# A weight stream split in two parts: moving the upper part from GpSimd to ScalarE

## The reference

```python
def reference(x, c, ctx, ...):
    x = first_block(x, c, ctx, ...)      # modulated norm; windowed attention with rope and
                                         # context, a gated convolution, gates, mixing; then
                                         # 8 heads pick 16 experts each of 16384 per token;
                                         # final rmsnorm
    return second_block(x, mem_2, ...)   # layer 0: mLSTM mixer; layer 1: pooling mixer;
                                         # each then attends to a memory of 256 rows and
                                         # runs a squared-ReLU MLP of width 4096,
                                         # a layer norm after every part
```

## Time and profile before

| | |
|---|---|
| median of 3 runs | 3497.38 us (3495.84 to 3499.48) |
| the profiled execution | 3496.58 us, its span 3494.8 us |
| mean granted TensorE clock | 0.928 of full speed |
| TensorE busy | 84% of the span |
| VectorE, ScalarE, GpSimd busy | 65%, 26%, 53% |
| DMA engines from 640 to 2000 us | near 100%, about 420 GB/s |

### The profile page before, as it was taken

The page is one execution under the profiler, slowest core; times in us unless marked ns, Lnnn a source line. Parts: engine busy times, 40 slices in busy tenths (PEclk is TensorE's granted clock), DMA queues, the critical chain, the costliest instruction groups (busy, mean ns, idle before and its releaser), DMA issues. The chain is left out here.

```text
span 3494.8 us, 33128 instructions
## 1 busy us (share of the span) xinstructions
PE 2945.1 (84%) x10628; PEld 1938.5 (55%) x10628; DVE 2257.4 (65%) x3761; ACT 926.1 (26%) x2350; POOL 1856.1 (53%) x1099
## 2 busy tenths in 40 slices
PE   6889898877778877888877779979899975889998
PEld 5667676632333323444433267657678864667886
DVE  7793464376666667776766583675855577586556
ACT  2115402233433333333333322221200012220001
POOL 2544375464444444666554264254577763557874
PEclk9899899999999999999999989989999987999998
DMA  5531122699999999999999811011122220112221
GB/s 216 185 113 55 43 79 73 241 421 419 413 418 412 412 422 409 391 389 399 390 422 418 341 66 55 31 60 61 60 90 96 91 72 12 61 60 93 94 96 55
DMA packets 126107, 719.21 MB, mean 206 GB/s; under 512 B 13200, under 2 KB 16400, under 8 KB 60176
## 3 DMA queue, kind: packets, MB, share of 16 engines
q0 software_dynamic: 73728, 536.90, 37.4%
q1 hardware_dynamic: 46560, 161.18, 13.4%
q10 hardware_dynamic: 5680, 19.40, 1.5%
HBM read 715.33 MB, written 2.10 MB: 205 GB/s over the span
## 5 line engine op out<-in xcount | busy, mean ns | idle before, releaser
L712 PE MATMUL psum<-slots,acc 128*128 128x512 f32 x2048 | 1016.2, 643 | 267.9 <-ACT acc L1167 267.4
L398 POOL TENSOR_TENSOR whi<-w,zeros 128x1024 fp32r<-128x1024 f32 x277 | 548.1, 1979 | 883.1 <-PE psum L469 566.4
L428 POOL DMA_INDIRECT slots<-in_experts,consts x512 | 564.1, 1102 | 675.0 <-PE psum L712 603.5
L1719 DVE SCALAR_TENSOR_TENSOR arena<-slots,work 128x1024 f32<-128x1024 f32 x512 | 663.2, 1295 | 400.1 <-DMA slots<-in_experts,consts 383.1
L712 PEld LDWEIGHTS psum<-slots,acc 128*128 128x128 f32 x2048 | 393.7, 202 | 868.5 <-ACT acc L1167 462.3
L401 POOL TENSOR_TENSOR wlo<-w,whi 128x1024 fp32r<-128x1024 f32 x277 | 718.2, 2593 | 21.7
L467 PE MATMUL psum<-xhi,whi 128*128 128x512 f32 x1104 | 451.5, 409 | 8.7 <-POOL wlo L401 5.6
L468 PE MATMUL psum<-xlo,whi 128*128 128x512 f32 x1104 | 441.8, 400 | 0.0
L469 PE MATMUL psum<-xhi,wlo 128*128 128x512 f32 x1104 | 440.5, 399 | 0.0
L467 PE MATMUL psum<-yhi,whi 128*128 128x512 f32 (+1 forms) x736 | 300.1, 408 | 49.9 <-POOL ylo L453 20.7
L468 PE MATMUL psum<-ylo,whi 128*128 128x512 f32 (+1 forms) x736 | 296.2, 402 | 0.0
(11 more groups left out here) (266 smaller groups left out, 3671.3 us busy)
## 6 DMA issues: line engine op xcount, KB each, us to landing
w<-in_stream SPq DMA_DIRECT2D x277, 512.0 KB
arena<-in_wmod SPq DMA_DIRECT2D x4, 2048.0 KB, 17.8
arena<-in_wmod ACTq DMA_DIRECT2D x8, 1024.0 KB, 6.1
acc<-in_wmod ACTq DMA_DIRECT2D x8, 1024.0 KB, 8.3
slots<-in_experts,consts POOLq DMA_INDIRECT x512
xres<-in_xT SPq DMA_DIRECT2D x1, 2048.0 KB, 15.3
outT<-xres SPq DMA_DIRECT2D x8, 256.0 KB, 2.0
consts<-in_consts SPq DMA_DIRECT2D x1, 1056.0 KB, 5.2
```

Of the source, the lines that this page charges most:

```text
L398: pool.tensor_tensor(hi, w32[:, s, :], zeros[:, :].broadcast_to((P, 1024)), ALU.add)\
L428: pool.indirect_dma_start(out=slots[p % SLOTS], out_offset=None, in_=a["experts"], in_offset=bass.IndirectOffsetOnAxis(ap=indices[:, p:p + ...
L712: mm = pe.matmul(bank(4 + half), diag[:, p % 2, :], v[:, half * T:(half + 1) * T], start=(c == 0), stop=(c == PICKS - 1))
L1719: dve.scalar_tensor_tensor(dot_out, slots[p % SLOTS][:, 0:D], 1.0, tokens[:, p // PICKS, :], ALU.mult, ALU.mult, accum_out=inner[:, c:c + ...
```

## The change

GpSimd no longer writes the upper part. ScalarE does, with a copy from `w32` into `whi`, and signals `w_upper`; the waits for the load and for `tile_done` move with it. GpSimd waits for `w_upper` to reach n + 1 and writes the lower part alone. Since ScalarE's list is written by hand, a call `upper(n + m + RING)` is put behind the instruction that reads product m in every stage: the upper part of a tile is written four tiles ahead, behind ScalarE's copy of the product of the tile whose slot it takes. In the start the first four uppers stand behind the root of the second norm.

```diff
-            def split_tile(s, n, nth, reused):
-
-                pool.wait_ge(w_loaded[s], nth * 16)
-                if reused:
-                    pool.wait_ge(tile_done, n + 1 - RING)
+            def split_tile(s, n):
+
+                pool.wait_ge(sem("w_upper"), n + 1)
                 hi = whi[:, s, :, :].rearrange("p k n -> p (k n)")
                 lo = wlo[:, s, :, :].rearrange("p k n -> p (k n)")
-                pool.tensor_tensor(hi, w32[:, s, :], zeros[:, :].broadcast_to((P, 1024)), ALU.add)\
-                    .then_inc(sem("w_upper"), 1)
-                pool.wait_ge(sem("w_upper"), n + 1)
                 pool.tensor_tensor(lo, w32[:, s, :], hi.bitcast(F32), ALU.subtract).then_inc(w_split, 1)
...
+            def upper(n, turn=0):
+
+                if n >= NTILES:
+                    return
+                s = n % RING
+                act.wait_ge(w_loaded[s], turn * 64 + 16 * (n // RING + 1))
+                if n >= RING:
+                    act.wait_ge(tile_done, turn * 16 + (n + 1 - RING))
+                act.activation(whi[:, s, :, :].rearrange("p k n -> p (k n)"), w32[:, s, :], ACT.Copy)\
+                    .then_inc(sem("w_upper"), 1)
...
                     act.activation(work[:, k % 2, 0:cols], src(k), ACT.Square).then_inc(sem("squared"), 1)
+                    if also is not None:
+                        also(k)
...
             root(1)
+            for m in range(RING):
+                upper(m)
...
             for i in range(5):
                 raw(i, o + 1 + i)
+                upper(n + i + RING)
...
                 attn_slot(i)
+                upper(SECTIONS[f"conv{i}"][0] + RING)
...
                 attn_slot(12 + i)
+                upper(n + i + RING)
             for i in range(28, 34):
                 attn_slot(i)
...
+            for m in range(KB):
+                upper(first_tile("branch") + m + RING)
...
+            squares(2, lambda k: xres[:, k, :], ready=lambda k: wait_read(act, SECTIONS["mix"][1] + k),
+                    also=lambda k: upper(first_tile("mix") + k + RING))
...
                         copy_product(mem_raw[:, m % 2, :], o + m, CT)
+                    upper(n + m + RING)
...
                 copy_product(lraw[:, m % 2, 3:3 + T], o + m)
+                upper(n + m + RING)
                 if m:
                     silu(m - 1)
...
+            def upper_after(n, per=1):
+                return lambda k: upper(n + k // per + RING) if k % per == per - 1 else None
+
+            n, o = SECTIONS["lout"]
+            post_norm(4, 0, read_of(o), also=upper_after(n))
...
-                    post_norm(7, 3, pooled)
+                    post_norm(7, 3, pooled, also=upper_after(n, 4))
...
                     copy_product(xq[:, m, :], oo)
+                    upper(n + m + RING)
                     if m % 2:
...
                 for k in range(4):
                     relu(o + k, layer == 0 and k < 2, k)
+                    upper(n + k + RING)
+
+                def hidden_group(half, turn):
+                    for k in range(4):
+                        relu(o + 4 + 12 * half + k, False, 4 + 4 * half + k, turn)
+                        upper(n + 4 + 8 * half + k + RING, turn)
+                    for k in range(4):
+                        upper(n + 8 + 8 * half + k + RING, turn)
+
                 with act.Fori(0, 3) as g:
...
+                post_norm(ni + 2, 3 * layer + 2, read_of(o + 88), last=(layer == 1), also=upper_after(n + 60, 2))
```

More of the change, by code:

```diff
@@ L980, in _, with squares @@
             step = Steps(act, "act_step")
-            def squares(ni, src, cols=T, ready=None):
+            def upper(n, turn=0):
[7 more added lines that the diff above has]
+                    .then_inc(sem("w_upper"), 1)
+            def squares(ni, src, cols=T, ready=None, also=None):
                 for k in range(KB):
@@ L1063, in _ @@
             act.activation(v_tok.rearrange("p t n -> p (t n)"), bank(7), ACT.Copy).then_inc(sem("values_copied"), 1)
+            upper(n + 5 + RING)
             def attn_exp(u):
@@ L1236, in _ @@
             act.activation(mrow, mrow, ACT.Ln, bias=1.0).then_inc(sem("gate_rows"), 1)
+            upper(n + 8 + RING)
             for m in range(9):
@@ L1241, in _ @@
                     copy_product(work[:, m % 2, :], o + 9 + m)
+                    upper(n + 9 + m + RING)
                 if m:
@@ L1264, in _ @@
                     free(act.activation(lsig[:, j, :], bank(oo % RING), ACT.Sigmoid), oo)
+                    upper(n + 2 * h + j + RING)
                 for j in range(2):
@@ L1270, in _, with post_norm @@
             head_root(3)
-            def post_norm(ni, j, ready, last=False):
-                squares(ni, lambda k: acc[:, k, :], ready=ready)
+            def post_norm(ni, j, ready, last=False, also=None):
+                squares(ni, lambda k: acc[:, k, :], ready=ready, also=also)
                 root(ni)
@@ L1286, in _ @@
                 if layer:
-                    o = SECTIONS["pool"][1]
+                    n, o = SECTIONS["pool"]
                     def scale_pooled(k):
@@ L1331, in _ @@
                 x_copy(3)
-                post_norm(ni + 1, 3 * layer + 1, read_of(SECTIONS[f"xo{layer}"][1]))
+                n, o = SECTIONS[f"xo{layer}"]
+                post_norm(ni + 1, 3 * layer + 1, read_of(o), also=upper_after(n))
                 act.wait_ge(sem("affine_done"), 8 * (ni + 2))
@@ L1351, in _ @@
                     relu(o + k, layer == 0 and k < 2, k)
-                with act.Fori(0, 3) as g:
-                    for half in range(2):
-                        for k in range(4):
-                            relu(o + 4 + 12 * half + k, False, 4 + 4 * half + k, g)
-                for k in range(4):
-                    relu(o + 76 + k, False, 28 + k)
-                post_norm(ni + 2, 3 * layer + 2, read_of(o + 88), last=(layer == 1))
+                    upper(n + k + RING)
[5 more added lines that the diff above has]
+                        upper(n + 8 + 8 * half + k + RING, turn)
+                with act.Fori(0, 3) as g:
+                    hidden_group(0, g)
+                    hidden_group(1, g)
+                hidden_group(0, 3)
+                post_norm(ni + 2, 3 * layer + 2, read_of(o + 88), last=(layer == 1), also=upper_after(n + 60, 2))
         @block.vector
```

14 lines of the change are left out of this document (6 added, 8 removed).

## The result

The changed kernel takes 3346.76 us (median of 4 runs, 3342.16 to 3349.42) beside 3496.61 us for the kernel before (4 runs, 3494.16 to 3499.48). The ratio is 0.957, with a 95% interval of 0.9553 to 0.9586: 150 us faster. The forecast was 3382, its range 3350 to 3442.

The account below looks back on a forecast made before the run. VectorE, slowed beside GpSimd's weight splits, was taken to delay the serial stages between stretches bound by TensorE or DMA. Stage terms summed to -115 us from 3497.4, giving 3382 us, range 3350 to 3442.

Parts of the forecast that it names:

- the LSTM: LSTM projections: three of VectorE's four instructions per tile become free, TensorE sets the pace; -19 us (-7 to -21).
- the MLP starts: Start of both MLPs: a hidden tile takes about 4.2 us on VectorE and TensorE's waits go; -20 us (-6 to -22).
- L1984's median: Sign: this 128x512 VectorE instruction's median falls from 1546 ns to near 700, its maximum staying near 2900.
- L583's wait: Sign: TensorE's wait for VectorE before the LSTM's value tiles, 15.3 us there, should go.
- L505's sum: Sign: TensorE's total wait for the sums of the later norms falls from 52.8 to about 22 us.
- L614's wait: Sign: TensorE's wait for the attention's turned probabilities, 29.1 us, falls to about half.
- the halving: Attention: half of 19 us of TensorE's waiting and some of the half clock after it go; -10 us.
- the bound of -17: Large end of the attention term, which was -10 us with bounds -4 to -17.
- the reading of the DMA share: Expert stage, between gathers: DMA at 0.98 against 1.00 read as 7 us lost; term -4 us (-12 to +5).
- half of it: Rival: each lower part hits VectorE's critical instruction, or two blocked instructions per tile remain; -50 us, 3447; chance 0.18.
- Slower: Rival: weights come late behind ScalarE where TensorE waits for a bank freed by a copy; +37 us, 3534; chance 0.06.
- the large ends together: All terms at their large bounds: -151 us, 3346 us; times below the range got chance 0.05.

Follow-up runs that it names:

- fills: Changed kernel with two GpSimd fills of 0.95 us and two one-column additions before each lower part, no tensor moved: 3384.5 us, ratio 0.969.
- repeated upper part: Changed kernel in which GpSimd writes the upper part again into the lower part's place before subtracting, for all tiles: 3456.3 us, ratio 0.9897.
- putting it back in this stretch alone: Changed kernel with GpSimd writing the upper part again for tiles 6 to 21 only (rotations, attention beside conv tiles): 3357.7 us, ratio 0.9617.
- the addresses: Kernel before the change with 4 unused bytes per partition behind `zeros`, moving the tensors behind it: 3475.6 us, ratio 0.9961.
- the order alone: Changed kernel, but ScalarE only signals with a one-column copy at its upper parts' places and GpSimd makes both parts: 3468.0 us, ratio 0.9932.
- pads of 0 and 60 bytes: Changed kernel with unused bytes per partition behind `zeros`: 0 gives 3346.8 us, 60 gives 3347.8; 4 gives 3323.4, 12 gives 3325.6.

## Why the prediction was right, and where it was wrong

Right was the mechanism and its place. VectorE was slow because GpSimd's reads blocked it; the change removes half of these instructions; the stages in which VectorE ends last gain. The pair of fills and repeated upper part is the test: with GpSimd held about as long and ScalarE's work the same, the instruction that reads cost 72 us more than the fills. The terms for the rotations, the LSTM, the norms, the cross attentions, the MLP starts and the pool are all within 3 us of what was measured, and of the signs named ahead all came but one: L1984's median fell to 694 ns, its maximum stayed, L583's wait went, L505's sum fell to 25.4 us (22 expected), ScalarE takes 1.05 us for a tile, the lower part holds TensorE for 4.4 us. The one that did not come is L614's wait, which was to fall to about half and fell to a quarter, 7.7 of 29.1 us.

The step that failed in the attention is the halving. The prediction said "Halving 19 us of waiting and some of the half clock after it". Half the blocked instructions need not leave half the wait. The term was 10 us for both attention stretches; 29.2 were gained, 27.2 of them beside the conv tiles. A stretch that VectorE bounds gets shorter with VectorE until TensorE bounds it, and here the change crosses that point: VectorE's busy time fell from 109.6 to 78.7 us against TensorE's 95.2. All of the waiting went, and with it all of the half clock. GpSimd's second instruction accounts for 11.1 of the 27.2 us, as putting it back in this stretch alone showed; the fills, which take as long and do not read the weights, give back 0.7. Where the other 16 us come from is open, the order and the addresses being worth some 5 to 6 each. Still, the trace of before had the end value. In its window above the granted clock is 0.91 over 122.3 us, 11 us lost, and the table of waits of that stretch has

```profile
PE psum L614 <- DVE arena L1553: 19.4, 6, 4.8
```

122.3 - 19.4 - 11 is 92 us, a possible gain of 30. This estimate is a few us too large, since part of the half clock ran while TensorE waited: TensorE was busy for 102.9 us, 7.7 more than the 95.2 at the full clock, and 122.3 - 19.4 - 7.7 is the 95.2 that came out. For the bound of -17 the prediction shows no working. For the LSTM and the MLP starts the prediction had done exactly this comparison, VectorE's time for a tile against TensorE's 5.6 us, and came within 1 us. That closeness is in part luck, as the next paragraph shows. A slip of its sum at the MLP start has no effect: at the 0.233 us of its own rows 5 us hold 21 matmuls, not 23.

The order has a share in the gain too, which the prediction took for nothing: 24 us in all. In the LSTM projections the order alone gives 9.6 us, half of the 19.1 that the prediction had put down to fewer blocked instructions. At the MLP starts the order alone costs 7.1 us, so the division of the work gave some 28 where 21 were measured and 20 forecast. The terms came out right as sums of two effects, one of which was not in the forecast: that is luck in the size, though not in the sign. How the two add up within a stage was not taken apart further.

The step that failed between the gathers is the reading of the DMA share. The prediction took 0.98 against 1.00 as 7 us of loss in 360. The column beside it in the earlier trace rows says 393 GB/s against 413, 5% and not 2%, which over 360 us is 17.4 us; 17.2 were gained, and the stretch now runs at 415 GB/s. That the two agree so closely is luck, for it hangs on the stretch that one compares with: over all of the first gathers, 640 to 1398 us, the kernel before moved 408 GB/s (and 404 from 640 to 2000, not the 420 of the table ahead), which gives 13 us. Between 392 and 415 GB/s the share moves only from 0.97 to 1.01. The cause was named rightly, a split in front of the gathers on GpSimd's queue: with fills, which do not block VectorE's instructions with two inputs, 9.4 of the 17.2 us came back, at 400 GB/s:

```profile
1362.60:1708.20 345.60, 285.37 (x906) 145.16 (x904) 234.84 (x516) 145.31 (x440) 225.22 (x203) 0.94 0.98 400
```

and with the repeated upper part 16.5, at 392. The 7 us between the two go with VectorE's blocked time; that they pass through its dot products, which feed the chain that frees the slots, is argued and not shown. The rule of the Trainium skill that I had weighed (SBUF — State Buffer, Who interferes with whom, Practical consequences: descriptor writing on GpSimd stalls behind VectorE's two-port instructions) would have made the term 0. The issue times here show no sign of such a stall: VectorE's busy time fell by 273 us, and the gathers are issued in the same time, 1102 ns on the mean before and 1096 after.

```profile
L423 POOL DMA_INDIRECT slots<-in_experts,consts x512 | 561.0, 1096 | 711.5 <-PE psum L707 648.5
```

Of the rivals, "half of it" was refuted by its own condition: one blocked instruction per tile did remain, mostly on the critical instruction (L1405, 55 of 68, 2373 ns on the mean), but VectorE's time for a tile still fell below TensorE's, and then it costs nothing. "Slower" would have cost some 10 us in its places when the order is changed alone, and nothing is left of that when VectorE gets faster; whether its mechanism was behind these 10 us is not shown. The range was too narrow below. It left out "the large ends together", whose sum, 3346 us, is close to the measured time by chance: most terms lay near their middle, and three went past their large end, the attention (29.2 us against 17), the expert stage (18.3 against 12) and, by 1 us, the norm after the LSTM.

Left open are the exact share of order and blocking within a stage, 16 of the 27.2 us of the attention beside the conv tiles, why the attention stretch takes 116.3 us with the order alone and 106.3 with the repeated upper part, where GpSimd reads SBUF equally often, and what the addresses do to the matmuls.

## What to carry to other kernels

An engine that is off the critical path can set the time through what it blocks: look for one instruction whose median is twice its minimum, and for what the engine beside it runs at that moment. When such a block is removed, price each stage by comparing the new busy time of the late engine with that of the next one, and let the whole wait go where it falls below; a fraction of the wait is right only where the late engine stays last. For a stretch that transfers bound, look at GB/s beside the busy share: here the rate rose by 6% while the share rose by 4%, and rounded shares of 0.98 and 1.00 had hidden a difference of 5%.

## What the hardware showed that was not expected

- Fills by GpSimd do not slow VectorE's instructions with two inputs from SBUF, and they do slow its casts from SBUF to SBUF. Beside fills alone 61 subtractions of 128x512 took 691 to 694 ns, as they do undisturbed, and eight casts of 128x512 took 1186 ns instead of 426. Beside a GpSimd instruction that reads SBUF both kinds reach 2500 to 2800 ns. In the kernel 277 reading instructions of 2.03 us cost 72 us more than 554 fills of 0.95 us.
- The stream of matmuls depends on where the tensors lie. In a loop in which TensorE never waits, at the full clock, 128x512 matmuls followed each other in 232.9 ns with pads of 0 and 60 bytes and in 228.7 with 4 and 12. It is worth 22 us in the changed kernel (12 against 60 bytes, measured side by side) and 14 in the kernel before.
- The granted clock was lower where TensorE waited more. In the attention stretch it was 0.91 with 19.4 us of waits for VectorE, 0.95 with 16.4, 0.97 with 7.6, and 1.00 with none.
